# Attention scores from stacked upper and lower halves in a hybrid attention and linear-attention layer

## What is computed

```python
def diff_attend(q, k, v, lam, mask):          # q (B,Tq,H,2,dk), dk = 64, H = 4
    s = jnp.einsum('bqhmd,bkhmd->bhmqk', q, k).astype(jnp.float32) * (DA_DK ** -0.5)
    if mask is not None:
        s = jnp.where(mask, s, -jnp.inf)
    p = jax.nn.softmax(s, axis=-1)
    a = p[:, :, 0] - lam * p[:, :, 1]         # two maps per head, m = 0 and 1
    return jnp.einsum('bhqk,bkhv->bqhv', a.astype(v.dtype), v)

# prompt: queries in blocks of 128; a key's chunk of 64 must not be later than the query's
mask = key_chunk[None, :] <= q_chunk[:, None]
# sample: 32 new queries over 32 new and 256 cached keys, no mask
```

## Time and profile before

| | |
|---|---|
| median of 3 runs | 951.71 us (951.21 to 952.03) |
| the profiled execution's own time | 950.71 us |
| its span | 948.9 us |
| granted TensorE clock, mean | 0.997 |
| TensorE (PE) busy | 913.2 us, 96% |
| VectorE (DVE) busy | 483.7 us, 51% |
| ScalarE (ACT) busy | 361.1 us, 38% |
| GpSimd (POOL) busy | 122.6 us, 13% |

### The profile page before, as it was taken

One profiled execution on the slowest core, in us unless ns is written; L12 is line 12 of the kernel. 1 busy time (PEld: TensorE's weight loads), 2 busy tenths in 40 slices (PEclk: granted clock), 3 DMA queues, 4 the chain that ended last, 5 costly groups with the idle time before them and its releaser, 6 DMA issues. The chain is left out here.

```text
span 948.9 us, 16606 instructions
## 1 busy us (share of the span) xinstructions
PE 913.2 (96%) x6657; PEld 831.7 (88%) x6657; DVE 483.7 (51%) x1092; ACT 361.1 (38%) x871; POOL 122.6 (13%) x210
## 2 busy tenths in 40 slices
PE   4999999999999999999999999999998999999997
PEld 3799999989999889999889899898997989988884
DVE  5523287741217766244653464456447676991223
ACT  6545354422335444144443344335335332430011
POOL 1001122210102222000000000000001103540000
PEclk9999999999999999999999999999999999999998
DMA  8012011213110203251132201221124225551222
GB/s 261 15 46 66 24 47 61 78 46 99 45 45 24 63 28 102 59 192 37 32 137 74 74 1 58 62 74 46 46 78 128 83 77 170 175 172 44 89 89 77
DMA packets 85837, 74.07 MB, mean 78 GB/s; under 512 B 4697, under 2 KB 78082, under 8 KB 85506
## 3 DMA queue, kind: packets, MB, share of 16 engines
q1 hardware_dynamic: 85762, 73.02, 25.3%
HBM read 53.29 MB, written 19.73 MB: 77 GB/s over the span
## 5 line engine op out<-in xcount | busy, mean ns | idle before, releaser
L1384 PE MATMUL proj_bank<-x_hi,w_hi 128*128 128x352 f32 x1056 | 350.5, 332 | 0.9 <-ACT feature_stage L867 0.9
L1386 PE MATMUL proj_bank<-x_hi,w_lo 128*128 128x352 f32 x1056 | 339.5, 322 | 0.0
L1385 PE MATMUL proj_bank<-x_lo,w_hi 128*128 128x352 f32 x1056 | 338.9, 321 | 0.0
L1384 PEld LDWEIGHTS proj_bank<-x_hi,w_hi 128*128 128x128 f32 x1056 | 198.5, 188 | 4.2 <-issue 1.5
L1385 PEld LDWEIGHTS proj_bank<-x_lo,w_hi 128*128 128x128 f32 x1056 | 199.0, 188 | 0.0
L1386 PEld LDWEIGHTS proj_bank<-x_hi,w_lo 128*128 128x128 f32 x1056 | 198.2, 188 | 0.0
L620 DVE TENSOR_TENSOR w_lo<-w_raw,w_hi 128x1024 fp32r<-128x1024 f32 x49 | 59.9, 1223 | 76.5 <-ACT w_hi L616 76.5
L977 ACT ACTIVATE probs<-score_banks,softmax_stats 128x128 f32<-128x128 f32 (+8 forms) x72 | 51.2, 712 | 77.9 <-DVE softmax_stats L1300 69.2
L1045 POOL TENSOR_TENSOR stats<-stats,minus_half 128x1 f32<-128x1 f32 (+1 forms) x36 | 22.3, 620 | 371.5 <-DVE stats L1333 371.5
L1030 POOL TENSOR_TENSOR decays<-log_decay 128x128 f32<-128x128 f32 (+1 forms) x122 | 47.8, 424 | 156.5 <-ACT log_decay L914 156.5
L616 ACT ACTIVATE w_hi<-w_raw 128x1024 fp32r<-128x1024 f32 (+1 forms) x53 | 55.1, 1040 | 15.6 <-PE proj_bank L1386 14.8
(11 more groups left out here) (180 smaller groups left out, 1402.1 us busy)
## 6 DMA issues: line engine op xcount, KB each, us to landing
w_raw<-in_w_in SPq DMA_DIRECT2D x44, 512.0 KB, 4.6
merge_tanh_scratch<-feature_stage SPq DMA_DIRECT2D x16, 528.0 KB, 3.0
feature_stage<-merge_tanh_scratch SPq DMA_DIRECT2D x10, 528.0 KB, 3.9
x_rows<-in_x_prompt SPq DMA_DIRECT2D x8, 512.0 KB, 6.7
w_raw<-in_w_out SPq DMA_DIRECT2D x8, 512.0 KB, 4.6
branch_out<-in_x_prompt SPq DMA_DIRECT2D x8, 512.0 KB, 3.6
out<-branch_out SPq DMA_DIRECT2D x8, 512.0 KB, 2.6
tokens_stage<-merge_tanh_scratch SPq DMA_DIRECT2D x6, 528.0 KB, 3.7
```

The lines of the kernel that those rows point to most:

```text
L1384: nc.tensor.matmul(out, wh, xh, start=first, stop=False)
L1385: nc.tensor.matmul(out, wh, xl, start=False, stop=False)
L1386: return nc.tensor.matmul(out, wl, xh, start=False, stop=last)
```

## The change

Six things change.
1. **Scores.** Keys are kept as `k_stacked` (float32r, 128 partitions, 2 maps): for map m, the upper part stands in its own 64 rows and the lower part in the other 64. Queries are made per step into `q_stacked` (128 x 4 x 128, two buffers): for map m, slice 2m holds q's upper part in both halves of the rows, slice 2m+1 the lower part in the map's own rows and zeros elsewhere. A bank of scores is then two float32r matmuls of 128 rows, q upper times (k upper + k lower) and q lower times k upper; map 0 is finished before map 1.
2. **Queries rounded mid-step** (stage `qd`): behind the first unit of step s, ScalarE makes four copies of 64x128 and VectorE two subtractions for the queries of step s+1; aS of s+1 waits for them on TensorE.
3. **Keys rounded** (stages `ks`, `kc`): the key tile leaves its bank into a feature stage; per third, two ScalarE copies and two subtractions of 64x352, for heads 1 to 3 at the end of the step (behind aQ, ahead of the next aS), for head 0 behind its unit. The cached keys go through their stage, two copies and two subtractions of 64x256 at the end of step i = 1.
4. **Mask.** The mask matmuls and their constant go. VectorE writes -1e30 into 64x64 of each map's bank before the maximum.
5. **Last projection tile.** Its matmuls with x's lower part come first, for thirds 0 and 1 together before unit 0 (`ulo`), for third 2 before unit 2; the units then have 16 matmuls each, of the upper part. After each `ulo`, `obload` loads that third of the branch straight into the place of x's lower part, and ScalarE and VectorE split it in place. The early load at step 9 and its stage go.
6. Sizes and places of buffers follow.

```diff
@@ unit, in stage_list
-        stages.append(("unit", t, th, 0))
+        if t < len(tiles) - 1:
+            stages.append(("unit", t, th, 0))
+        else:
+            for n in ((0, 1), (), (2,))[th]:
+                stages.append(("ulo", t, n))
+                stages.append(("obload", n))
         if later:
             stages.append(later.pop(0))
         stages.append(("unit", t, th, 1))
+        if kind == "dk" and i:
+            keys.append(("ks", i, th))
+        elif kind == "dk":
+            stages.append(("ks", i, th))
@@ step, in stage_list
             unit(*u)
+            if n == 0 and at_step(s + 1):
+                stages.append(("qd",) + at_step(s + 1))
...
         if two:
             stages.append(("aQ",) + two)
+        stages.extend(keys)
+        keys.clear()
+        if now and now[1] == 1:
+            stages.append(("kc", now[0]))
@@ ScalarE
+            def keys_hi(h, cols, src, s_hi):
+                for m in range(2):
+                    r = slice(64 * m, 64 * m + 64)
+                    last = nc.scalar.activation(t_["K"][h % 2][r, m, cols], src[r, :], ACT.Copy)
+                last.then_inc(s_hi, 1)
...
+                elif kind == "qd":
...
+                    if s >= 2:
+                        act.wait_ge(s_sc, 2 * (s - 1))
...
+                    for m in range(2):
+                        for e in (m, 1 - m):
+                            last = nc.scalar.activation(t_["QD"][s % 2][64 * e:64 * e + 64, 2 * m, 0:n],
+                                                        t_["Q"][h % 2][64 * m:64 * m + 64, tok(i)], ACT.Copy)
+                    last.then_inc(s_qdh, 1)
@@ VectorE
+            def keys_lo(h, cols, src, s_done):
+                for m in range(2):
+                    r, other = slice(64 * m, 64 * m + 64), slice(64 - 64 * m, P - 64 * m)
+                    K = t_["K"][h % 2]
+                    last = nc.vector.tensor_tensor(K[other, m, cols], src[r, :], K[r, m, cols].bitcast(F), ALU.subtract)
+                last.then_inc(s_done, 1)
...
                         dve.wait_ge(s_sc, 2 * s + m + 1)
+                        if i < TT:
+                            w = nk - 64
+                            link(nc.vector.memset(SC[0:64, 2 * m + w // 512, w % 512:w % 512 + 64], BIG))
                         link(nc.vector.reduce_max(mm[:, m:m + 1],
...
+                elif kind == "qd":
...
+                    dve.wait_ge(s_qdh, s + 1)
+                    for m in range(2):
+                        r = slice(64 * m, 64 * m + 64)
+                        last = nc.vector.tensor_tensor(QD[r, 2 * m + 1, 0:n], Q[r, tok(i)], QD[r, 2 * m, 0:n].bitcast(F),
+                                                       ALU.subtract)
+                    last.then_inc(s_qd, 1)
@@ TensorE, aS
-                    nb = -(-nk // 512)
-                    for b in range(nb):
-                        w = min(512, nk - 512 * b)
-                        cc = slice(c0 + 512 * b, c0 + 512 * b + w)
-                        masked = i < TT and b == nb - 1
-                        done = [None, None]
-                        for m in range(2):
-                            r = slice(64 * m, 64 * m + 64)
-                            if s and b == 0:
-                                pe.wait_ge(s_ex, 2 * s - 1 + m)
-                            done[m] = nc.tensor.matmul(SC[0:n, 2 * m + b, 0:w], t_["Q"][h % 2][r, tok(i)],
-                                                       t_["K"][h % 2][r, cc], start=True, stop=not masked)
-                        for m in range(2) if masked else ():
-                            r = slice(64 * m, 64 * m + 64)
-                            done[m] = nc.tensor.matmul(SC[0:n, 2 * m + b, w - 64:w], t_["MR"][r, 0:P],
-                                                       t_["MR"][r, P:P + 64], start=False, stop=True)
+                    pe.wait_ge(s_qd, s + 1)
+                    QD, K = t_["QD"][s % 2], t_["K"][h % 2]
                     for m in range(2):
-                        done[m].then_inc(s_sc, 1)
+                        if s:
+                            pe.wait_ge(s_ex, 2 * s - 1 + m)
+                        for b in range(-(-nk // 512)):
+                            w = min(512, nk - 512 * b)
+                            keys = K[:, m, c0 + 512 * b:c0 + 512 * b + w]
+                            out = SC[0:n, 2 * m + b, 0:w]
+                            nc.tensor.matmul(out, QD[:, 2 * m, 0:n], keys, start=True, stop=False)
+                            last = nc.tensor.matmul(out, QD[:, 2 * m + 1, 0:n], keys, start=False, stop=True)
+                        last.then_inc(s_sc, 1)
```

More of the change, by code:

```diff
@@ L124, in stage_list @@
     stages = []
-    later, branch, carried = [], [], []
+    later, branch, carried, keys = [], [], [], []
     def whole(kind, i):
@@ L219, in stage_list @@
         unit(*u)
+        if n == 0:
+            stages.append(("qd", 0, 0))
         if n < 2:
@@ L314, in hybrid_kernel @@
     NP_ = len(tiles)
-    ft_tiles = [t for t, (k, _, _) in enumerate(tiles) if k not in ("ga", "gk", "gq", "dq", "dk")]
+    ft_tiles = [t for t, (k, _, _) in enumerate(tiles) if k not in ("ga", "gk", "gq", "dq")]
     ft_no = {t: n for n, t in enumerate(ft_tiles)}
@@ L427, in attention @@
             low = dict(
-                GATE=[al(f"da_gate{s}", [P, T]) for s in range(2)], Q1=al("da_q1", [P, T]), K1=al("da_k1", [P, KC]),
+                QD=[al(f"q_stacked{s}", [P, 4, P], R) for s in range(2)],
+                GATE=[al(f"da_gate{s}", [P, T]) for s in range(2)], Q1=al("da_q1", [P, T]), K1=al("k_stacked1", [P, 2, KC], R),
                 V1=al("da_v1", [P, NTT + 2, DV]),
@@ L523, in hybrid_kernel @@
         s_lame = sem("lambda_exp")
-        s_obld = sem("gla_branch_loaded")
+        s_obld = [sem(f"gla_branch_loaded{th}") for th in range(3)]
         s_bh = sem("gla_branch_hi")
@@ L1422, in _ @@
                             pe.wait_ge(s_uout, u - 1)
-                    for k in range(KD_ // 2 * st[3], KD_ // 2 * (st[3] + 1)):
+                    for k in range(KD_ // 2 * st[3] if t < NP_ - 1 else 0, KD_ // 2 * (st[3] + 1)):
+                        if t == NP_ - 1:
+                            nc.tensor.matmul(bank, w_hi[t % 2][:, k, :], XH[:, k, cols], start=False, stop=False)
+                            last = nc.tensor.matmul(bank, w_lo[t % 2][:, k, :], XH[:, k, cols], start=False, stop=k == KD_ - 1)
+                            continue
                         if t < 2:
@@ L1434, in _ @@
                         last.then_inc(s_unit, 1)
+                elif kind == "ulo":
+                    t, th = st[1], st[2]
+                    u = unit_no(t, th)
+                    if th == 0:
+                        pe.wait_ge(s_wlo, t + 1)
+                    pe.wait_ge(s_uout, u - 1)
+                    for k in range(KD_):
+                        last = nc.tensor.matmul(PJ[u % 2][:, 0:TH], w_hi[t % 2][:, k, :], XL[:, k, TH * th:TH * (th + 1)],
+                                                start=k == 0, stop=False)
+                    last.then_inc(s_xldone, 1)
                 elif kind == "bunit":
@@ L1481, in _ @@
                     pe.wait_ge(s_uout, units_done(t))
-                    x = t_["K"][tiles[t][1] % 2] if tiles[t][0] == "dk" else FT[ft_no[t] % NFT]
+                    x = FT[ft_no[t] % NFT]
                     take()
```

107 lines of the change are left out of this document (72 added, 35 removed).

## The result

The changed kernel takes 991.34 us (median of 4 runs, 987.71 to 992.76) against 951.71: a ratio of 1.041, interval 1.0385 to 1.0434. It is slower, as forecast, but by more than twice as much, and outside the range. The profiled execution took 992.0 us, with a span of 990.2 and a mean granted TensorE clock of 0.981 (before: 948.9 and 0.997).

The account below looks back on a forecast made before the run. The prediction took TensorE, busy 96% of the span, as the bound: -7.3 + 12.0 + 1.5 + 3.3 + 8.2 + 0.3 = +18.0 us on the profiled 950.71, hence 969 us for the median of runs; range 953 to 980.

Parts of the forecast that it names:

- The score blocks, -8.8: Attention score matmuls on TensorE: blocks shorten by 2.2 us per head over four heads, mostly from the missing mask matmuls.
- the floor: Score matmuls below some 240 columns were taken to start no closer than 0.11 us apart, the distance of two transposes.
- the entry: Start of each score block after a transpose: taken as unchanged; the skill's tiling-mode rule would save 3.3 us more.
- The queries' waits, 12.0 + 1.5: Score blocks waiting for rounded queries: 12.0 us behind six single units, 1.5 us in step (3,5).
- the chain: Queries' rounding before a score block: four ScalarE copies, two VectorE subtractions and semaphore hops, 1.75 us, bounds 1.0 to 2.3.
- Memsets and key stages on VectorE, 3.3 + 8.2: VectorE late ahead of token transposes: 3.3 us from mask memsets, 8.2 us from key rounding in four steps.
- the six steps that the prediction named: Steps (0,4), (0,7), (1,3), (1,7), (2,3), (2,6): memset waits before token transposes, 3.0 us together.
- paid in full: Any wait put before a TensorE instruction costs its own length, since its instructions follow each other without a gap.
- The recurrence, 0.3 with bounds 0 to 3: Head 0's three key stages lie in the recurrence, covered by two units per chunk: 0.3 us lost.
- a chunk there has two units over it: In the recurrence, two projection units per chunk were to cover head 0's key stages, leaving 0.3 us.
- The last projection, 0: Same 72 matmuls reordered, 0 us; each branch third lands in about 4 us, its load hidden.
- The rival "more": Late branch thirds, key stages holding the recurrence, or late exponentials delaying evacuations: 10 us more, 979 us; chance 0.12.

Follow-up runs that it names:

- Experiment 1: Changed kernel with the queries' rounding stage moved ahead of the step's first unit: 975.96 us, ratio 1.0265 to the kernel before.
- Experiments 2 and 7: 2: changed kernel, key stages moved behind the next step's transposes, 981.14 us. 7: changed kernel, queries' and key stages both moved, mask left out, 962.92 us.
- Experiment 9: Kernel before, plus only a dummy copy and subtraction chain that six score blocks wait for: 970.47 us, ratio 1.0189.
- experiment 3: Changed kernel with thrown-away matmuls filling TensorE's wait ahead of six score blocks: 985.71 us, ratio 1.0353 to the kernel before.
- experiment 6: Changed kernel with queries' and key stages both moved, and head 0's key stages put off to the next unit's start: 970.31 us, ratio 1.0198.
- experiment 5: Kernel before with only the last projection's part of the change (x's lower part first, branch in thirds, rounded in place): 952.38 us, ratio 1.0017.
- experiment 10: On experiment 6, queries' stage early only before single units, first third's lower part and load earlier, key stages behind token transposes: 961.7 us, ratio 1.0108.
- experiment 11: On experiment 10, the chunk mask added by one TensorE matmul per map, no memset: 957.28 us, ratio 1.0062 to the kernel before.

## Why the prediction was wrong

The span grew by 41.3 us; the sum said 18.0. By its own steps:

- **The score blocks, -8.8: right, a little small.** The matmuls start 0.11 to 0.23 apart, as read. From the start of the transpose ahead to the start of aV, 256 keys in (1,1) took 1.00 us and now 0.67; 896 keys in (2,6) took 2.08 and now 1.74; the sample tile, without its waits, 0.88 and now 0.80, not the 0.14 gained that the floor gave. Over the nine tiles of a head that is 2.3 to 2.8 us, 9.9 in all (waits left out, and the four blocks at half clock put at what the same tile takes in another head or run). In the entry the transpose is mostly followed after 0.03 us instead of 0.20, and the first float32r matmul of 512 columns takes 0.32 instead of 0.23. The Trainium skill (TensorEngine Tiling (Array Packing), Key Properties) has a change of tiling mode drain TensorE, from which I had worked out 3.3 us more. The blocks as measured gave 1.1 us more than the 8.8.
- **The queries' waits, 12.0 + 1.5: right.** Seven waits, of 2.4 (three), 1.8 to 1.9 (three) and 1.4 us, 14.1 in all. Experiment 1 took six of them away. In part this is luck: in (0,6) the four copies took 1.26 us, not 0.9, and the two subtractions 0.59, not 0.8, so that two errors in the chain nearly cancel.
- **Memsets and key stages on VectorE, 3.3 + 8.2: right as waits.** The list has 12.7: 2.9 in (0,6), 3.3 in (2,5), 1.9 in (1,6), 1.4 in (2,2), where the prediction had 2.7, 2.3, 1.6, 1.6, and 0.6 to 0.7 in five others, 3.2 in all. Of these five only four are among the six steps that the prediction named; (0,7) and (1,7) have no such wait, and (0,3), which it excepted, has one: the 3.3 came out partly for other steps, by luck. Experiments 2 and 7 took the two kinds away one after the other. Too small was what stands behind them, next.
- **The granted clock: the step that failed; it is no term of the sum.** I read the clock on the page (0.997), saw the half clock only at the span's end, where TensorE has nothing left to do, and counted every wait at its own length: "paid in full", and nothing behind it. In the changed kernel 34.1 us ran at half clock, some 16.4 us lost: the largest single item. The waits of before in the attention are at most 1.0 us, so its trace showed no price; but it did show the lower level, and so a stretch at half rate behind each of the ten waits that I forecast at 1.6 us or more belonged into the range. At the 1.7 us lost in one, as now measured, that is 17 us, and the range would have held the time. Experiment 9 shows it with nothing but waits, experiment 3 by filling them. The Trainium skill (TensorE: Matmul & The Clock Gate, HAM oscillation — how this bites in real kernels) describes a kernel that waits for loads and falls back to the slower clock each time. This case agrees in kind, with waits of 1.8 to 3.3 us for other engines.
- **The recurrence, 0.3 with bounds 0 to 3: wrong step, "a chunk there has two units over it".** The units cover ScalarE and VectorE's sum, not their order: 2.6 us in one wait of the output product, and a stretch at half clock behind it. The attention starts 4.8 us late; experiment 6 gave back 3.5 of it.
- **The last projection, 0: "hidden" was wrong in company, right alone.** A third lands in 7.1 us, not 4. Alone it costs 1.6 us (experiment 5). In the changed kernel steps (3,4) to (3,6) take 40.0 us instead of 33.5: the late exponentials, the query copies and the memsets all stand on the same two engines. The rival "more" names this and the recurrence, and stops at 979, since it too leaves out the clock.

The pieces: -9.9 blocks, +14.1 queries, +12.7 token waits, +16.4 clock, +2.3 recurrence, +2.5 in the waits of L1476 for the last copy and the branch, +2.7 more in the waits for the combined probabilities (L1713, where the prediction had 1.5 as gain not realised): 40.8 of 41.3. That it comes so near is partly luck, since other small waits grew by 1.6 us more; the account is good to about 2 us.

What stays open: why three of the eleven long waits had no half clock behind them and a cluster of waits of about 1 us had (experiment 10). Over the traces of the changed kernel and all experiments, 35 of 48 waits of 1.8 us or more, from 300 us on, have a stretch that begins during the wait or at most 1.5 us behind it, or that covers it; the same 2.60 us in the recurrence has one in five of the six traces that hold it. So the stretch is a chance, not a certainty, and nothing here says what decides it. Whether a version that mixes memset and matmul by step would reach the kernel before was not tried: taking for each step the shorter of experiments 10 and 11 gives 2.4 us less than experiment 11, which would still be slower than before.

## What to carry to other kernels

On a kernel that TensorE bounds, a wait has two prices: its length, and in most cases a stretch at half clock behind it, 1.7 us, which here nearly doubled the smaller ones. So count the waits that a change makes as well as their sum, and prefer three hidden stages to one that stands in front of TensorE by 2 us. A stage put on "idle" engines (54% and 42% busy here) costs by its place in their order: what stood ahead of an operation for which the bound engine waits was paid here, and most of the rest was hidden. Placing the queries, the keys and the last projection's first third differently, and giving the mask back to TensorE, gave back 34 of the 40 us.

## What was unexpected of the hardware

- The granted clock fell from 2.4 to 1.2 GHz behind single waits of TensorE of 1.8 to 3.3 us, within a span of otherwise full work, for 3.41 us in most cases, 6.83 or 10.24 in some: 8 of 11 waits in the changed kernel, 5 of 6 in the profiled execution of experiment 9. In no trace did a wait of 1.0 us or less that stood by itself do it.
- A copy on half the partitions costs ScalarE about as much as on all: 297 ns for 64x128 against 316 for 128x128. VectorE's subtraction took 275 ns there, against 447 for 128x128, which I had taken. (Both means hold some shorter ones, of 32 columns.)
- A memset of 64x64 in a score bank takes 112 ns; the row of 256 columns has 272.
- A 704 KB load into the branch's place took 7.1 us (6.8 in experiment 5), the whole 2112 KB 10.3 before: a third of the bytes is two thirds of the time. (The third is read in runs of 352 columns, the whole in full rows; how much of the time that makes was not tested.)
